# Moving fourteen modulation pieces from the first layer's attention into the gated linear attention of the second

## The reference

```python
for layer in range(DEPTH):                      # first block
    if layer % 2 == 0:
        a = _mla(...); r = _retention(...)      # even: 16 (tile, head) pairs of attention, then retention
        x = x + concatenate([a, r]) @ w_out_even
    else:
        g = _gla(...)                           # odd: A = mask(qc kc^T); o = A v + q' S, both directions
        x = x + g @ w_out_odd
    x = x + _conv_ffn(x, ...)
# second block: mod = silu(cond) @ w_mod + b_mod, for two conditionings, six parts of 1024 columns a layer
```

## Time and profile before

| what | us |
|---|---|
| median of 3 runs (2591.42 to 2592.03) | 2591.72 |
| the profiled execution, its own time | 2591.42 |
| its span in the profile | 2589.6 |
| TensorE busy | 2420.3 (93%) |
| VectorE busy | 1769.0 (68%) |
| ScalarE busy | 1260.7 (49%) |
| attention of the even layer | about 115 to 167 |
| odd layer up to its output projection | about 424 to 559 |

### The profile page before, as it was taken

One profiled execution on the slowest core, in us unless ns is written; L12 is line 12 of the kernel. 1 busy time (PEld: TensorE's weight loads), 2 busy tenths in 40 slices (PEclk: granted clock), 3 DMA queues, 4 the chain that ended last, 5 costly groups with the idle time before them and its releaser, 6 DMA issues.

```text
span 2589.6 us, 36327 instructions
## 1 busy us (share of the span) xinstructions
PE 2420.3 (93%) x13802; PEld 2025.4 (78%) x13824; DVE 1769.0 (68%) x1887; ACT 1260.7 (49%) x1457; POOL 523.6 (20%) x407
## 2 busy tenths in 40 slices
PE   7999999989999988879999979889999999999997
PEld 5658998769997855658889967578788788887886
DVE  6556865467855766467655357658888888888886
ACT  5444343544443365322222134536767667676674
POOL 1003541004512000030003420002232232232221
PEclk9999999999999998889999989888999999999998
DMA  5574554414552200125555323026989889899894
GB/s 196 196 271 144 180 184 144 159 53 148 185 190 90 101 25 1 49 94 199 195 195 196 107 81 107 1 84 260 345 323 359 341 336 352 335 342 354 326 361 173
DMA packets 71468, 503.73 MB, mean 195 GB/s; under 512 B 8192, under 2 KB 8704, under 8 KB 11264
## 3 DMA queue, kind: packets, MB, share of 16 engines
q1 hardware_dynamic: 70128, 496.75, 52.4%
q0 software_dynamic: 1168, 4.66, 0.5%
HBM read 500.33 MB, written 1.05 MB: 194 GB/s over the span
## 4 chain that ended last, share of the span: by engine, by line
PE 83%; DVE 10%; ACT 4%; issue 2%; POOL 1%; DMA 0%; DVEq 0%; ACTq 0%; SPq 0%; PEldq 0%
PE ps L417 79%; DVE ring_r L2092 1%; DVE h L2070 1%; PE ps L457 1%; POOL h_r L1344 1%; DVE h L2068 1%; DVE areaA L2062 1%; PE ps L1168 1%; DVE h L2072 1%; ACT ring_hi L1461 1%; ACT h L1539 1%; DVE areaB L2584 1%; DVE temp L2155 0%; DVE h L2669 0%; PE ps L560 0%
## 5 line engine op out<-in xcount | busy, mean ns | idle before, releaser
L1461 ACT ACTIVATE ring_hi<-ring 128x2048 fp32r<-128x2048 f32 x427 | 807.4, 1893 | 578.0 <-PE ps L417 353.4
L2841 DVE TENSOR_TENSOR ring_r<-ring,ring_hi 128x2048 fp32r<-128x2048 f32 x264 | 628.9, 2388 | 115.6 <-ACT ring_hi L1461 114.6
L417 PE MATMUL ps<-ring_hi,extra_r 128*128 128x512 f32 (+2 forms) x1808 | 610.2, 394 | 35.1 <-DVE ring_r L2092 20.3
L2092 DVE TENSOR_TENSOR ring_r<-ring,ring_hi 128x2048 fp32r<-128x2048 f32 (+3 forms) x163 | 383.2, 2351 | 196.8 <-ACT ring_hi L1461 181.8
L417 PE MATMUL ps<-extra_r,ring_hi 128*128 128x256 f32 (+1 forms) x1432 | 462.2, 323 | 21.8 <-POOL h_r L1344 20.4
L417 PE MATMUL ps<-extra_r,ring_r 128*128 128x256 f32 (+1 forms) x1432 | 457.8, 320 | 0.0
L417 PE MATMUL ps<-h_r,ring_hi 128*128 128x256 f32 (+2 forms) x1400 | 445.5, 318 | 0.0
L417 PEld LDWEIGHTS ps<-ring_hi,extra_r 128*128 128x128 f32 x1808 | 343.0, 190 | 111.7 <-DVE ring_r L2092 23.7
L417 PE MATMUL ps<-ring_r,extra_r 128*128 128x512 f32 (+2 forms) x1104 | 426.0, 386 | 0.0
L417 PEld LDWEIGHTS ps<-extra_r,ring_hi 128*128 128x128 f32 x1432 | 273.9, 191 | 45.2 <-POOL h_r L1344 23.4
L417 PEld LDWEIGHTS ps<-extra_r,ring_r 128*128 128x128 f32 x1432 | 273.7, 191 | 19.2
(11 more groups left out here) (356 smaller groups left out, 3236.8 us busy)
## 6 DMA issues: line engine op xcount, KB each, us to landing
ring<-in_experts SPq DMA_DIRECT2D x264, 1024.0 KB, 4.9
ring<-in_stream SPq DMA_DIRECT2D x202, 1024.0 KB, 4.9
ring<-in_stream SPq DMA_DIRECT2D x6, 512.0 KB, 3.7
ring<-in_stream SPq DMA_DIRECT2D x2, 576.0 KB, 3.7
res<-in_xT SPq DMA_DIRECT2D x1, 1024.0 KB, 6.1
res<-in_ctxT POOLq DMA_DIRECT2D x1, 1024.0 KB, 7.3
h<-in_consts POOLq DMA_DIRECT2D x2, 512.0 KB, 4.7
areaB<-in_cond_rows POOLq DMA_DIRECT2D x1, 1024.0 KB, 5.9
```

Source lines behind the costliest of these rows:

```text
L417: return pe.matmul(o, l, r, start=start, stop=stop, skip_group_check=True)
L1461: return act.activation(dst, src, ACT.Copy)
L2092: L.tell(TTN(ring_lo[:, s, 0:n], ring[:, s, 0:n], ring_hi[:, j % HIS, 0:n].bitcast(F32), ALU.subtract), "weights_lo")
L2841: TTN(ring_lo[:, s, :], ring[:, s, :], ring_hi[:, j % HIS, :].bitcast(F32), ALU.subtract).then_inc(sig("weights_lo"), 1)
```

## The change

There are 20 fills as before, and their order is the same. In attention only heads 2 and 13 keep one. The four of retention stay. Fourteen fills are moved to five places of the odd layer: one behind its sum of squares, two between gla_b(1) and the last projection, one at the end of each of the eight passes of the loop, and three between the last gla_o and the last turnings. On ScalarE the counterparts stand behind `hi_upto(j + 2)`, behind `hi_upto(j + 14)`, at the end of each pass, and behind the second root. The order of the chunks on SP's queue follows TensorE's program, so the 14 loads of 1 MB move too.

```diff
--- before.py
+++ after.py
@@ -102,7 +102,8 @@
 HALVES = [16, 8]
 MOD_PIECES = 20
 
-FILL = {"attention": 16, "ret": 4}
+MLA_FILL = (2, 13)
+FILL = {"attention": len(MLA_FILL), "ret": 4, "odd": 1, "gla_gates": 2, "gla": 8, "odd_mix": 3}
 
 MOD_COLUMNS = [(0, c) for c in range(MOD_PIECES, 24)] + [(1, c) for c in range(24)]
 PARTS = {"even_act": 0, "even_dve": 0, "odd_act": 7, "odd_dve": 5}
@@ -668,7 +669,8 @@
                 for n in range(len(MLA)):
                     if n + 2 < len(MLA):
                         scores(n + 2)
-                    fill(1)
+                    if n in MLA_FILL:
+                        fill(1)
                     turn_p(n)
                     if n:
                         pv(n - 1)
@@ -891,6 +893,7 @@
 
 
             sum_squares("odd")
+            fill(FILL["odd"])
             first_split["odd_in"] = len(splits)
             h_split(1)
 
@@ -961,6 +964,7 @@
                     full(mm(ps[:, u.bank, :], glam[:, 3 * d + 2, :], la[:, d, t, :]), u)
             gla_b(0)
             gla_b(1)
+            fill(FILL["gla_gates"])
             tokens("odd_in", ("w_in_odd", 0), 6, ODD["v"] + 512, ODD["r"])
 
             pe.wait_ge(sig("gla_kdT"), 4)
@@ -987,9 +991,11 @@
                 full(m, u)
                 if n and d == 0:
                     gla_o(x - 1)
+                fill(FILL["gla"] // (2 * GH))
             for fp in range(2):
                 turn_mix("odd", po, fp, 8)
             gla_o(GH - 1)
+            fill(FILL["odd_mix"])
             for fp in range(2, 4):
                 turn_mix("odd", po, fp, 10)
             out_project("odd_out", ("w_out_odd", 0), 1, 2 * (MIXED["odd"] + TT), "ffn1", True)
```

## The result

The kernel after takes 2604.88 us (median of 6 runs, 2599.67 to 2612.74) against 2591.60 for the kernel before beside it: a ratio of 1.0051, interval 1.0037 to 1.0064. It is slower, by 13.3 us of the medians; forecast was +2.5, and the time lies above the range (2586 to 2602). The profiled execution took 2603.11 us, 11.7 above that of before. The six runs of the kernel after spread over 13 us where the six of before spread over 2. Over all runs on record the kernel after stands between 2599.41 and 2612.74 (27 runs), and the kernel before, taken again beside the experiments, within 8 us (2588.81 to 2596.90).

What follows compares the result with a forecast made beforehand. TensorE was busy nearly throughout attention and the loop; without fills a ring through three engines would bound attention. Terms -13.1 + 0 + 5.0 + 8.2 + 2.4 = +2.5 us: 2594.2 median, range 2586 to 2602.

Steps and rivals of the forecast that it cites:

- the ring: Attention: dependent chain through VectorE's decays, ScalarE's decay and exp, scores and copy sets 4.54 us for two heads, 2.27 each.
- the granted clock in attention falls: Sign of being wrong: TensorE's clock in attention drops below the 1.00 that the forecast expected.
- The slower rival: Thinned attention loses full clock: 5.1 us a pair, 6.0 with retention turnings, 7.8 us more, total 2602.0; chance 0.20.
- The last rival: Attention's removed work is partly covered, heads stay near 3 us: +12, total 2604; chance 0.10.
- Forecast for attention: Attention without 14 fills, from scores(2) to the copy of head 15: 35.5 us against 48.65, -13.1 us.
- gla_gates: Two fills behind gla_b(1): the second waits 2.8 us for bank 7; +5.0 us, +2.2 without that wait.
- The loop: Eight fills in the gated attention's loop: 11.7 us of TensorE, partly hidden in idle time; +8.2 us.
- odd_mix: Three fills ahead of the last turnings: second waits for bank 7, a 1 us idle time of TensorE; +2.4 us.
- Loads: Moved 1 MB loads on SP's queue: over 5 us left before ScalarE wants the output projection's chunks; cost 0.
- odd: Fill behind the odd layer's sum of squares hides in 2.13 us of TensorE idle; 0, at most 1.5 without cover.

Runs made afterwards that it cites:

- thin_warm: thin_only plus three keep-warm matmuls of constants in each attention head without a fill; 2579.65 us, ratio 0.9952.
- thin_only: Kernel after without the 14 moved fills (their modulation columns set to zero, their chunks not loaded); 2586.81 us, ratio 0.9975.
- turns5: Kernel after with five extra transposes of a constant, results unused, in each attention head without a fill; 2601.51 us, ratio 1.0039.
- odd1: Kernel before with one fill moved, from attention head 15 to behind the odd layer's sum of squares; 2591.87 us, ratio 1.0002.
- decay_later: warm3 with ScalarE's exponential of the decays moved from the odd head to the even head behind it, behind exp; 2593.53 us, ratio 1.0011.
- warm3: Kernel after with three keep-warm matmuls in each attention head without a fill, all 20 fills computed; 2599.28 us, ratio 1.0030.
- warm3_gates: warm3 with ScalarE's part of the two fills behind gla_b moved ahead of its rounding of the last weight chunk; 2597.67 us, ratio 1.0025.
- mix_warm: warm3_gates plus eight keep-warm matmuls on TensorE in the stop behind the first of the three odd_mix fills; 2592.21 us, ratio 1.0002.
- gates_early: Kernel after with only ScalarE's part of the two fills behind gla_b moved ahead of its rounding of the last weight chunk; 2603.68 us, ratio 1.0037.
- best1: alternate with ScalarE's decays moved to the even heads as in decay_later; 2580.60 us, ratio 0.9959.
- alternate: All 20 fills: attention keeps them in odd heads and head 14, three norms one each, loop three, odd_mix one; against kernel before 2584.50 us, ratio 0.9974.

## Why the prediction was wrong

**The step that failed** is the condition under which the ring was priced: "2.27 each", with "a clock of 1.00". It named its own sign of being wrong, "the granted clock in attention falls", and that is what happened. The slower rival had the mechanism and got 0.20. (The last rival had the number, 2604, with another mechanism, heads that stay near 3 us; they took 2.3 to 2.5 where they had no fill.) Forecast for attention was -13.1; the kernel after got -5.8, 7.3 less, and the rival's price was 7.8. By copies of even heads the miss lies in the two pairs with a fill (6.99 us from 118.38 to 125.37 where 5.14 was forecast, and 6.15 where 4.4 was, 3.6 together), in the pairs at the lower clock without one (5.08 for 4.54, three of them, 1.6), 0.3 in a pair at full clock, and in the step behind attention (1.75). I had the rival's 5.1 for a pair right, its 6.0 with the turnings for retention not: the two of those pairs that ran at the lower clock took 5.08 too, and the other two ran at the full one. That the 7.8 came out near is luck: the turnings cost less than it had, and the two fills that stay cost nearly twice as much and the step behind attention 1.75 more, which I hadn't priced. That the cause is the clock, and that the clock follows from too little work, is shown by thin_warm against thin_only, with the profile of turns5 as a second way of filling the heads.

Why I chose wrongly: the row that I set against the rival, 545.8 to 559 us at 63% busy with a clock of 1.00, is a place with few, long gaps after a full loop. The row for it, 1000 to 1020 us at 0.74, is a string of short heads with a gap in each, which is what the thinned attention becomes. The second resembles the case; I gave the first as much weight. And the first doesn't even repeat: behind the loop odd1 runs the same instructions with the same stop, and its matmuls behind the stop are slow, in

```profile
553.21 1.00 PE L500 MATMUL ps<-cst,areaA 128*128 128x128 f32 x4 [3.24 <-DVE areaA L2497]
```

against 0.66 in the earlier trace rows. The window from 543 to 558 us, which holds this stop in all three, has a clock of 1.00 in the kernel before and 0.89 in odd1 and in thin_only.

**The ring** was right in its parts and its size: 4.55 against 4.54 in the one pair at full clock that it bounds alone, with ScalarE's decay and exp on the chain, and decay_later confirms it. The other pair at full clock took 4.86, with VectorE's scaling of the first eight heads on the chain, which the sum didn't have.

**"gla_gates"**: +8.1 for +5.0. The term missing is what the clock does behind a stop: 3.1 us, from warm3 against warm3_gates, which is all of the miss. The rest came out right as a sum of two errors that cancel: the wait was priced at 2.8 and the new order took 2.0 away (2.42 to 0.42), and without the wait I had said +2.2 where it was +2.95.

**The loop**: +8.85 for +8.2, right; it is full. **"odd_mix"**: +2.7 for +2.4, right, with the stop ended by ScalarE's copy as forecast; it is longer than was said (1.87 us, forecast 1). **Loads**: 0, right. **"odd"**: odd1 shows no cost (1.0002). The -2.0 of the stretch there, the +1.6 of the feed-forward before it and the -1.6 of the rest nearly cancel; pieces of that size come and go in stretches that an edit doesn't touch, so no fill is charged with them. From 230 to 235 us, in the feed-forward, the granted clock of the kernel after was 0.66, though nothing had been changed there. What starts such a loss is open.

Where the profile's 9.2 us of miss lie: attention 7.3, gla_gates 3.1, loop 0.65, odd_mix 0.3, and -2.1 of untouched stretches. The median is some 2 us higher still, since the runs spread: those of about 2600 us had a mean clock of 0.964, those of about 2604 had 0.961, and that of 2612.74 had 0.957. Each 0.003 to 0.004 of mean clock goes with 4 to 9 us.

**Would the change ever pay?** With the clock held at all three places (mix_warm) the median is that of before. The profile says what is behind that: attention gives 10.5 and the three places of the odd layer take 14.5 (2.9, 8.9 and 2.7), a net loss of 4 us; stretches that the edit doesn't touch are 3.4 us shorter than in the profile of before, and they are of the kind that comes and goes. Where the work is only moved, a full receiver such as the loop takes about what the donor gives. It pays to move few, from where one is left beside each gap, into stops of TensorE that exist anyhow.

## What to carry to other kernels

Filler work in a stage of short dependent steps does two jobs: it gets done, and it holds TensorE's clock. Before taking it out, price what is left at the lower level too, fills that stay included, and look in the trace for a stage with the same pattern of gaps, not the same busy share. Work whose result goes through a single buffer must be counted in its consumer's program order: two in a row behind a long operation mean a stop, and a stop can cost the clock on top.

## What the runs showed of the hardware

- Stops of the same length didn't do the same to the clock. After 1.87 us in odd_mix it held in the kernel after, warm3 and decay_later and fell in gates_early, warm3_gates and (a fill later) turns5; after 2.42 us at gla_gates it fell. The idle 3.23 us of the kernel before left a window clock of 1.00, and behind the same stop the clock fell in odd1 and thin_only, with the same instructions around it. No single length of stop separates these, and each is one profiled execution.
- The kernel after spreads most: 13 us, in groups that go with its mean clock. How far a kernel spreads doesn't follow from keep-warm matmuls alone: thin_warm has them and spreads over 1.3 us, mix_warm over 3.4, but decay_later, with the same ones in its heads, over 6.6; best1, with none, over 5.
- With five transposes or three keep-warm matmuls in each head without a fill (0.55 and 0.65 us of TensorE by their starts, in heads of 2.4 us) the profiled clock from 118 to 150 us was 1.00; with nothing in their place it was 0.70. With a fill in nearly every second head it was 1.00 in best1 and 0.95 in alternate.
